# Expert phase of a two-layer diffusion backbone: codes of two steps in one table load, indices a step earlier, gate turned later

## What is computed

```python
def expert_block(args):
    tok, e = args
    xb = xpad[tok]
    h = jax.nn.silu(xb @ w1[e]) * (xb @ w3[e])
    return h @ w2[e]

yb = lax.map(expert_block, (slot_tok.reshape(n_blocks, EBLK), block_e))
routed = jnp.zeros((t + 1, d), xt.dtype).at[slot_tok].add(yb.reshape(n_slots, d) * slot_w[:, None])[:t]
```

## Time and profile before

| | us |
|---|---|
| median of 3 runs | 3729.34 |
| the runs | 3728.5, 3729.34, 3734.95 |
| profiled execution | 3735.04 |
| its span, first to last instruction | 3732.9 |
| TensorE busy | 3077.4 (82%) |
| VectorE busy | 2092.6 (56%) |
| ScalarE busy | 1595.8 (43%) |
| GpSimd busy | 611.4 (16%) |

### The profile page before, as it was taken

One profiled execution on the slowest core, in us unless ns is written; L12 is line 12 of the kernel. 1 busy time (PEld: TensorE's weight loads), 2 busy tenths in 40 slices (PEclk: granted clock), 3 DMA queues, 4 the chain that ended last, 5 costly groups with the idle time before them and its releaser, 6 DMA issues. The chain is left out here.

```text
span 3732.9 us, 59388 instructions
## 1 busy us (share of the span) xinstructions
PE 3077.4 (82%) x12317; PEld 2076.6 (56%) x12318; DVE 2092.6 (56%) x3692; ACT 1595.8 (43%) x2328; POOL 611.4 (16%) x609
## 2 busy tenths in 40 slices
PE   5698999996768888888888299887658888888884
PEld 0245667754346666666666244454426666666663
DVE  0334433334367767667657521386347777787575
ACT  0133222222036656556646311243116666676564
POOL 0000000000013333333332000000002333333331
PEclk8796555577779999999999699999779999999997
DMA  9701000003059989887878510100318899999785
GB/s 403 279 0 48 1 1 1 1 1 123 23 206 309 287 249 301 268 254 247 259 211 286 167 46 23 48 1 1 112 55 289 276 310 305 285 311 325 229 279 174
DMA packets 137601, 652.76 MB, mean 175 GB/s; under 512 B 24104, under 2 KB 31912, under 8 KB 80424
## 3 DMA queue, kind: packets, MB, share of 16 engines
q1 hardware_dynamic: 93312, 526.56, 36.6%
q0 software_dynamic: 43200, 121.69, 16.5%
q10 hardware_dynamic: 1000, 3.41, 0.2%
HBM read 594.85 MB, written 92.37 MB: 184 GB/s over the span
## 5 line engine op out<-in xcount | busy, mean ns | idle before, releaser
L1454 PE MATMUL e_psH<-e_w13h,e_xh 128*128 x1184 | 580.1, 490 | 109.5 <-DVE e_w13l L1636 88.9
L1636 DVE TENSOR_TENSOR e_w13l<-ring,e_w13h x512 | 603.4, 1221 | 103.9 <-ACT e_w13h L1542 77.4
L1542 ACT CAST e_w13h<-ring x512 | 509.9, 1044 | 171.7 <-issue 105.0
L1454 PE MATMUL e_psH<-e_w13l,e_xh 128*128 x1184 | 480.9, 406 | 0.0
L1623 DVE TENSOR_TENSOR e_w2l<-ring,e_w2h 128x1024 fp32r<-128x1024 f32 x256 | 302.3, 1222 | 158.5 <-ACT e_w2h L1531 158.5
L1454 PEld LDWEIGHTS e_psH<-e_w13h,e_xh 128*128 128x128 f32 x1184 | 230.2, 194 | 223.6 <-issue 180.5
L455 PE MATMUL psP<-ring,ho 128*128 128x512 f32 x800 | 349.5, 592 | 0.0
L1440 PE MATMUL e_psT<-m_id,e_xg 128*128 128x128 f32 x1184 | 325.5, 277 | 6.8 <-DMA e_xg<-h_rows,e_gidx 4.6
L1460 PE MATMUL e_psH<-e_w13h,e_xl 128*128 x1184 | 310.6, 404 | 0.0
L1397 POOL DMA_INDIRECT y_rows<-e_y,e_sidx x148 | 241.9, 1634 | 345.6 <-ACT e_y L1568 330.4
L1440 PEld LDWEIGHTS e_psT<-m_id,e_xg 128*128 128x128 f32 x1184 | 228.9, 194 | 61.5 <-DMA e_xg<-h_rows,e_gidx 4.8
(11 more groups left out here) (266 smaller groups left out, 4506.3 us busy)
## 6 DMA issues: line engine op xcount, KB each, us to landing
ring<-in_exp_w SPq DMA_DIRECT2D x388, 1024.0 KB, 7.4
ring<-in_ada_w SPq DMA_DIRECT2D x48, 1024.0 KB, 13.2
ring<-in_c_w_in SPq DMA_DIRECT2D x6, 2048.0 KB, 14.7
bc<-mod_rows SPq DMA_DIRECT2D x4, 1536.0 KB, 8.3
r_bc<-mod_rows SPq DMA_DIRECT2D x4, 1536.0 KB
ring<-in_sh_w SPq DMA_DIRECT2D x6, 1024.0 KB, 13.3
h_rows<-r_hrow SPq DMA_DIRECT2D x10, 512.0 KB, 2.6
y_rows<-r_y SPq DMA_DIRECT2D x10, 512.0 KB, 2.6
```

The costliest lines, as they stand in the source:

```text
L1454: nc.tensor.matmul(psH[par][:], xh[par][:, k * P:(k + 1) * P], w[:, bass.DynSlice(half, 1), :, k, :], start=(k == 0 and i == 0), stop=False)
L1542: nc.scalar.copy(w13h[:, bass.DynSlice(half, 1), :, k, :].rearrange("p o u k n -> p (o u) (k n)"), raw13[:, bass.DynSlice(half, 1), :, k, ...
L1636: nc.vector.tensor_tensor(low, raw, high.bitcast(F32), ALU.subtract).then_inc(w13_lo, 1)
```

## The change

On PE, ACT and DVE, the single reads of a code are replaced by one read of several neighbouring codes (6 or 7 on PE, 4 on ACT, 7 on DVE) before the loop and at the top of each loop body; steps get them as arguments. PE no longer reads the expert's row of the table; it takes the expert from the code. SP still reads its entries singly. On PE, `turn_gate(b-1)` stands in `hidden(b)` after k=2, where `turn_gate(b)` stood in `down(b-1)`. On ACT and DVE all four pieces of `split13` and `rest13` stand together. On ACT `rows_out(b-1)` comes before `gate(b)`. On DVE `choose(b+5)` comes directly behind `product(b)`, and `indices(b+4)` (before: `indices(b+3)`) behind `rest13(b+2)`.

```diff
-        expert_of = lambda eng, b: entry(eng, 0, b, E - 1)
-        code_of = lambda eng, b: entry(eng, 1, b, 8 * E * E - 1)
+        def codes(eng, b, n):
+
+            return nc.values_load_multi_w_load_instructions(r.table[0:1, bass.DynSlice(b + P, n)], engines=[eng.engine], min_val=0,
+                                                            max_val=8 * E * E - 1)[1]
+
...
-            def index(b, par, e):
-
+            def index(b, par, code):
+
+                e = expert_in(code)
...
-            def down(b, par, code, first, second):
+            def down(b, par, code, between):
...
                     if k == 0:
-                        first()
+                        between()
...
-                    if k == 0:
-                        second()
...
-            def step(b, m, par, first=False):
-
-                code, e = code_of(pe, b), expert_of(pe, b + 4)
-                before = None if first else code_of(pe, b - 1)
-                hidden(b, par, code, lambda k: turn(b + 1, m, 1 - par, k))
+            def step(b, m, par, before, code, later, first=False):
+
+                def beside(k):
+                    turn(b + 1, m, 1 - par, k)
+                    if k == 2 and not first:
+                        turn_gate(b - 1)
+
+                hidden(b, par, code, beside)
...
-                    down(b - 1, 1 - par, before, lambda: index(b + 4, par, e), lambda: turn_gate(b))
+                    down(b - 1, 1 - par, before, lambda: index(b + 4, par, later))
...
             with pe.Fori(0, n - 1) as i:
-                step(2 * i + 2, i + 1, 0)
-                step(2 * i + 3, i + 2, 1)
+                code = codes(pe, 2 * i + 1, 7)
+                step(2 * i + 2, i + 1, 0, code[0], code[1], code[5])
+                step(2 * i + 3, i + 2, 1, code[1], code[2], code[6])
...
-            def step(b, par):
+            def step(b, par, code, later):
 
                 rows_in(b + 1, 1 - par)
                 silu(b, par)
-                split13(b + 2, range(2))
-                gate(b, par)
+                split13(b + 2, later)
                 if not isinstance(b, int) or b > 0:
                     rows_out(b - 1, 1 - par)
-                split2(b)
-                split13(b + 2, range(2, PIECE))
+                gate(b, par)
+                split2(b, code)
...
-            def step(b, par):
+            def step(b, par, code, later, latest):
 
                 rows_in(b + 1, 1 - par)
                 product(b, par)
-                indices(b + 3)
-                choose(b + 5, 1 - par)
-                rest13(b + 2, range(2))
+                choose(b + 5, 1 - par, latest)
+                rest13(b + 2, later)
+                indices(b + 4)
                 gate(b, par)
-                rest2(b)
-                rest13(b + 2, range(2, PIECE))
+                rest2(b, code)
```

More of the change, by code:

```diff
@@ L1515, in _ @@
             m = ending(pe)
-            code, before = code_of(pe, m + 2), code_of(pe, m + 1)
-            hidden(m + 2, 0, code, lambda k: None)
-            down(m + 1, 1, before, lambda: None, lambda: turn_gate(m + 2))
-            down(m + 2, 0, code, lambda: None, lambda: None)
+            code = codes(pe, m + 1, 2)
+            hidden(m + 2, 0, code[1], lambda k: turn_gate(m + 1) if k == 2 else None)
+            down(m + 1, 1, code[0], lambda: None)
+            turn_gate(m + 2)
+            down(m + 2, 0, code[1], lambda: None)
@@ L1539, in split13 @@
                     wait_for(act, h_mm, b - 1)
-                    for j in pieces:
+                    for j in range(PIECE):
                         k = slice(j * KP, (j + 1) * KP)
@@ L1624, in rest2, with rest13 @@
                                                 ALU.subtract).then_inc(w2_lo, 1)
-            def rest13(b, pieces):
-                code = code_of(dve, b)
+            def rest13(b, code):
                 with dve.If((code & 7) == 0):
                     o, half = order_in(code), half_in(code)
-                    for j in pieces:
+                    for j in range(PIECE):
                         k = slice(j * KP, (j + 1) * KP)
```

65 lines of the change are left out of this document (32 added, 33 removed).

## The result

| | before | after |
|---|---|---|
| median | 3728.92 (4 runs) | 3683.01 (4 runs, 3672.43 to 3689.78) |
| profiled execution, its span | 3735.04, 3732.9 | 3680.0, 3677.0 |
| TensorE busy | 3077.4 | 3012.7 |

The ratio is 0.9873, 95% interval 0.9845 to 0.9901: 46 us faster, where 115 were forecast. The time lies inside the range and outside the forecast's own part of it (3545 to 3664); it falls into the rival "the waits come back elsewhere" (3650 to 3700).

The account below looks back on a forecast made before the run. TensorE was taken to set the step, with the DMA hardly 3% behind. Per stretch, the larger of DMA share plus 0.03 and TensorE at 0.90 gave gains of 74 and 41, together 115 us: 3614 us, range 3535 to 3700.

Parts of the forecast that it names:

- the waits come back elsewhere: Rival, chance 0.18: read at the jump costs by the entry, gap 1.92 us, w2's rest perhaps late; 3650 to 3700 us.
- Indices a step ahead: TensorE's wait ahead of the index product, 0.98 and 0.91 us a step, goes: 136 us of idle time.
- Codes: Reads between a pair's steps go, with 0.57 us; the bulk read leaves 1.16 us at the jump, at most 2.4.
- TensorE's floor: TensorE's need in each step: 0.855 of today's without waits, 0.90 with the 1.16 us left at the jump.
- The upper end: Slow end of the forecast: DMA hand-over 0.06, TensorE at 0.94 of the step; gain 65 us, 3664 us.
- The DMA floor: DMA work in a step with a new expert: 8.05 us of weights plus 3.96 of gathers and scatters, 12.0 us.
- The DMA gives way: Rival, chance 0.10: packets get shorter when asked for sooner; step at 0.88 everywhere, 218 us gained, 3511 us.
- The gate's turn: Two small transpositions move into the next step; about 1 us of slack for w2's rest, priced at nothing.
- Weight loads: Both loads leave together about 10 us after the cast; landing in 12 to 14 us, they fit at 12.39 us.
- slower case: Rival, chance 0.09: loads held behind w2 land in 16.5 us, steps with new experts take 13.25 us; 3786 us.
- Outside the loops: Outside the 146 steps of both layers' loops little is changed, so the gain is that of the steps.
- The clock: If the DMA makes new long waits in dense stretches, each costs about 1.4 us; counted in the upper end.

Follow-up runs that it names:

- e9_singles: Changed kernel with each read of several codes replaced by as many single checked reads in the same place; 3924.47 us, ratio 1.0493.

## Why the prediction was off

**Indices a step ahead: right, and more than forecast.** 136 us of waits were named, and no index wait is left. Undone alone it costs 154 us. The part "late next at that place is nothing" held. What the forecast missed is the refill with the stop, 0.6 to 0.8 us of busy time a step.

**Codes: the term that was mis-sized.** "I take the 1.16 us that stand there, the nearest row", with 2.4 as the upper bound. Measured 2.67 on average and 2.9 mostly. It fails twice. First, it priced reads by the idle time that they showed and not by what they take. "Its price has no row" was not so: the three reads between two steps of the kernel before take 2.9 us from the first load to the next product, 0.65 to 0.8 us from one load to the next, and 0.57 us of idle time shows only because 2.1 us lie under products in front. Seven such reads would take 5.9 us (`e9_singles` does), 4.3 more than the 1.6 us that can lie in front; such a bound would have held 2.9. The bound of 2.4 took two single reads for seven codes. Second, the prediction costs the load and never mentions the fourteen check instructions behind it, which are 2 of the 2.9 us.

**The rival "the waits come back elsewhere" was right in kind:** the gap grows with the entries, with w2's rest late as well. It had 1.92 us at the jump for 2.67, from 0.19 us an entry, which is again idle time: a checked code more takes about 0.5 us (0.24 in the load, 0.28 for the check). The Trainium skill's rule in "Runtime: NRT & Kernel Launch", section "Instruction fetch mechanics" (200 ns a register even in bulk, an estimated 1.4 us for seven), is near the load's own row: 1.70 us for seven on TensorE, 0.24 each. It is not the price of the read as the kernel writes it, which has the checks and the register work behind it.

**TensorE's floor: mis-sized the other way.** The sum put TensorE at 0.90 of the old step, from 0.855 plus the gap. The 0.855 was busy time, which held the refill of two stops a step and the stretches at the lower clock. A step without a stop takes 9.77 us, 0.76 and 0.79 of the old ones. The upper end has a slip of its own: with a gap of 2.4 us TensorE needs 0.855 + 1.2 / 12.6 = 0.95 of the step and not 0.94, which makes the least gain 55 us and not 65.

**The DMA floor: right.** It was 12.0 us for a step with a new expert. In a dense stretch of the changed kernel, 3180 to 3400 us (queues with packets, MB, share of 16 engines; issues with landing time):

```profile
q1 hardware_dynamic: 7608, 55.38, 66.8%
q0 software_dynamic: 5184, 14.40, 31.2%
...
ring<-in_exp_w SPq DMA_DIRECT2D x54, 1024.0 KB, 6.5
```

54 loads are 18 experts in 220 us: (0.668 + 0.312) x 220 / 18 = 11.98 us. "The DMA gives way" (3511) did not happen: the kernels near that time are there because the steps outside the dense stretches fell to what the DMA allows, at a share of 0.93 to 0.96.

**The sum again with the measured terms.** Same method and stretches. TensorE at the jump: (2 x 9.77 + 2.67 for the gap + 0.64 for w2's rest, 47.1 us over 73 pairs + 0.6 for the two refills) / 2 = 11.73 us, 0.92 and 0.95 of a step. Layer 0: 4 + 10 + 4 + 34 + 8 = 60; layer 1: 6 + 2 + 2 + 0 + 12 = 22; 82 us, and 65 were measured in the loops. The sum has no term for the clock, which lacks some 24 us more than before. With no gap only the DMA bounds (share plus 0.03): 4 + 20 + 4 + 77 + 12 = 117 and 10 + 2 + 7 + 0 + 38 = 57, 174 us. In the kernel without checks the first activations run from 1089.0 to 1925.7 and from 2684.9 to 3487.5 us, 836.7 and 802.6 us: 135 + 65 = 200 us gained. The method gives each time within 26 us; the two errors worked against each other, and 115 was neither. That the measured time lies inside the range at all is due to that.

**The gate's turn** was priced at nothing, and nothing was seen (0.9446 against 0.9452), though only where the DMA ends the step. W2's rest, however, came late, with a wait of about 1 us in 46 of 73 pairs. It does not hang on the checks: every version with the indices a step ahead has the wait (10 to 86 us in the loops, 59 for the order with its old checked reads, 86 for it without checks), and neither the kernel before nor the three versions that wait for the indices within the step have one in the loops. In these the index wait stands ahead of it in `down` and can hide it. Which part of the new order makes w2's rest late, the gate behind four casts or w2 as VectorE's last work, no run separates.

**Weight loads.** They leave together as forecast and land in 6.5 us at the median instead of 7.6, so the slower case (loads held behind w2) had no ground. **Outside the loops** the forecast expected little; 10 us were lost.

**The clock.** "Each costs about 1.4 us" was fair: a step with a stretch at the lower level has about 1.6 us more of busy time here. But the forecast looked for new waits at the DMA. They came at the jump, and the stretches at the lower level went from 27 steps to 44.

## What to carry to other kernels

Price a register read from the sequencer's own rows, together with the instructions that follow it, and take off what work stands in the engine's stream in front of it: the idle time in front of the next matmul shows only the rest. Six spread reads cost less here than one read of seven at a loop's top, since each place had its own cover. Read only the entries that are used, or drop the check where the writer of the table clamps it. When waits are to be removed, take the engine's floor from a stretch that has no stop in it and runs at the full clock; the step less its idle time understates what removing stops gives. Then ask which other resource is already at 0.9.

## What the runs showed of the hardware

- A load of codes into registers takes TensorE's stream 0.30 us for one, 0.54 for two, 0.77 for three and 1.70 for seven; a range check adds 0.28 us for each. From the load to the next product it is 4.5 us for seven checked codes, 2.5 unchecked, 3.7 for five in two loads and 5.9 for seven single ones. 1.6 to 1.7 us of that lie under products in the stream at most jumps; the rest is idle time. On VectorE a load of seven took 1.0 or 1.6 us at most places; what decides is not shown.
- A stop of TensorE costs busy time beside its idle time: 0.6 to 0.8 us at the index product, 0.25 us at a step's start. Four small matmuls take 0.26 us in the stream and 0.58 us behind a wait.
- Stretches at the lower clock level lie in 44 steps of the changed kernel, in 42 of them around a gap at the jump (mean 2.67 us), and add about 1.6 us of busy time to a step. In the version with gaps of 4.3 us the granted clock is 0.92 and 0.91, for 0.96 and 0.98 before.
- The work of the DMA engines stayed nearly the same at either pace: share times length of both loops is 0.85 x 972 + 0.90 x 868 = 1607 us before and 0.88 x 924 + 0.91 x 850 = 1587 us after.
